# A third buffer for the expert weights, in the place of the normed rows, which are read back from DRAM; expert loops six long

## What is computed

```
h  = x @ W_in                                       # columns for HGRN2 heads and FoX heads
x  = LN1(alpha*x + W_out[HGRN2(h_hg) | FoX(h_fx)])
x  = LN2(alpha*x + MemCrossAttn(x, mem))            # 4 heads, 256 memory tokens
x  = LN3(alpha*x + HierMoE(x))
```

```
h = silu(xr @ w_gate[e]) * (xr @ w_up[e])           # 1024 -> 512, twice
y = h @ w_down[e]                                   # 512 -> 1024
```

## Time and profile before

| | us |
|---|---|
| median of 3 runs | 1876.02 |
| lowest and highest | 1871.96, 1881.76 |
| the profiled execution | 1861.41 |
| its span | 1859.6 |
| PE busy in the span | 1744.6 (94%) |
| VectorE busy | 745.7 (40%) |
| ScalarE busy | 326.0 (18%) |
| GpSimd busy | 195.9 (11%) |

### The profile page before, as it was taken

The page is one execution under the profiler, slowest core; times in us unless marked ns, Lnnn a source line. Parts: engine busy times, 40 slices in busy tenths (PEclk is TensorE's granted clock), DMA queues, the critical chain, the costliest instruction groups (busy, mean ns, idle before and its releaser), DMA issues. The chain is left out here.

```text
span 1859.6 us, 34670 instructions
## 1 busy us (share of the span) xinstructions
PE 1744.6 (94%) x15263; PEld 1095.6 (59%) x15263; DVE 745.7 (40%) x1172; ACT 326.0 (18%) x741; POOL 195.9 (11%) x190
## 2 busy tenths in 40 slices
PE   7999999999999999989998999849999999999976
PEld 4555566655666654445665666536666666666652
DVE  0212456623866753320003433574444433344337
ACT  1111224410344211110001111100111100111115
POOL 2100000000422000000000000032111111111003
PEclk9999989999999999989999999869999999999998
DMA  6171002001002040154101000349999999999957
GB/s 211 45 235 46 1 1 94 1 1 48 1 5 96 3 150 35 50 185 152 45 0 46 23 23 23 146 172 373 423 425 425 425 424 424 425 425 425 414 209 277
DMA packets 72870, 322.32 MB, mean 173 GB/s; under 512 B 14464, under 2 KB 29112, under 8 KB 59728
## 3 DMA queue, kind: packets, MB, share of 16 engines
q1 hardware_dynamic: 47840, 280.70, 37.6%
q10 hardware_dynamic: 17360, 22.03, 3.7%
q0 software_dynamic: 7584, 18.38, 2.7%
HBM read 288.05 MB, written 37.65 MB: 175 GB/s over the span
## 5 line engine op out<-in xcount | busy, mean ns | idle before, releaser
L852 PE MATMUL psum<-arena 128*32 128x256 f32 x6144 | 339.9, 381 | 20.8 <-issue 14.0
L852 PEld LDWEIGHTS psum<-arena 128*32 128x32 f32 x6144 | 230.7, 110 | 128.6 <-issue 33.8
L457 PE MATMUL psum<-arena 128*128 128x512 f32 x656 | 292.1, 604 | 7.6 <-DMA arena<-in_w_in 6.5
L1456 DVE COPY arena<-psum 128x512 f32<-128x512 f32 (+6 forms) x128 | 83.8, 663 | 382.9 <-PE psum L457 225.7
L457 PEld LDWEIGHTS psum<-arena 128*128 128x128 f32 x656 | 125.6, 194 | 160.5 <-issue 158.6
L672 PE MATMUL psum<-arena 128*128 128x352 f32 x576 | 177.9, 460 | 0.0
L861 PE MATMUL psum<-arena 128*32 128x256 f32 x3072 | 172.3, 379 | 0.5 <-DVE arena L1906 0.5
L442 PE MATMUL psum<-arena 128*128 128x352 f32 x576 | 172.3, 462 | 0.0
L1165 ACT ACTIVATE arena<-psum 128x128 f32<-128x128 f32 (+7 forms) x193 | 94.2, 497 | 351.3 <-PE psum L435 250.2
L442 PEld LDWEIGHTS psum<-arena 128*128 128x128 f32 x576 | 110.3, 192 | 61.8 <-issue 1.7
L861 PEld LDWEIGHTS psum<-arena 128*32 128x32 f32 x3072 | 116.3, 110 | 50.1 <-DVE arena L1906 1.0
(11 more groups left out here) (271 smaller groups left out, 1565.6 us busy)
## 6 DMA issues: line engine op xcount, KB each, us to landing
arena<-in_moe_w_down SPq DMA_DIRECT2D x34, 2048.0 KB, 21.8
arena<-in_moe_w_gate SPq DMA_DIRECT2D x34, 2048.0 KB, 16.6
arena<-in_moe_w_up SPq DMA_DIRECT2D x34, 2048.0 KB, 21.3
arena<-in_w_in SPq DMA_DIRECT2D x7, 2048.0 KB, 10.1
y_blocks<-arena ACTq DMA_DIRECT2D x136, 96.0 KB, 27.3
y_blocks<-arena ACTq DMA_DIRECT2D x1, 8448.0 KB, 46.0
arena<-in_x_prompt SPq DMA_DIRECT2D x9, 512.0 KB, 3.2
arena<-in_w_out SPq DMA_DIRECT2D x2, 2048.0 KB, 7.8
```

The costliest lines, as they stand in the source:

```text
L457: last = mm(ps[0:n, c * 512:(c + 1) * 512], lhs(k), rhs(k)[:, c * 512:(c + 1) * 512], start=(k == 0), stop=(k == KD - 1))
L852: last = mm(out, xeT[:, b, a, k, :], gu[b][:, :, k, j * P:(j + 1) * P], start=(k == 0), stop=(k == KD - 1))
L1456: take(V.tensor_copy(out, src), key)
```

## The change

Three weight buffers stand where two stood. The third begins at 24576 and ends at 36864, so it covers the last 512 floats of the mixer's region, all of `x1` and the norm parameters behind it. Expert e uses buffer e mod 3 for its weights; the buffers of its activations still alternate. The weights of expert 2 are loaded once the second norm's output is stored in DRAM and the last tile of it is transposed. Gate and up of expert e are issued when `gate_up` of expert e - 3 is done. When `down` of expert 29 is done, SyncE reads the rows back from `x2_dram` into `x1`, ahead of the overflow blocks' weights, and VectorE's tail waits for them (`x1_back`). Since two and three buffers repeat after six, the loops on TensorE and SyncE hold six experts (8 to 31, four rounds), with experts 0 to 7 written out. The small expert buffers and the LN3 parameters move.

```diff
-        EXP = [0, 12288]
+        EXP = [0, 12288, 24576]
...
-        ln3_par = view(R + 17920, "i n", i=2, n=D)
+        ln3_par = view(R + 23552, "i n", i=2, n=D)
...
+        x1_back = sem("x1_back")
...
-            def step(e, b, j, first=False):
+            def step(e, r, third_turn, first=False):
+                b, s = r % 2, r % 3
                 if not first:
                     pe.wait_ge(xt_ready, e + 1)
-                pe.wait_ge(wg_in[b], 16 * j + 16)
-                pe.wait_ge(wu_in[b], 16 * j + 16)
+                pe.wait_ge(wg_in[s], 16 * third_turn(r) + 16)
+                pe.wait_ge(wu_in[s], 16 * third_turn(r) + 16)
...
-            step(0, 0, 0, first=True)
-            step(1, 1, 0)
-            step(2, 0, 1)
-            with pe.Fori(1, NE // 2 - 1) as i:
-                step(2 * i + 1, 1, i)
-                step(2 * i + 2, 0, i + 1)
-            step(NE - 1, 1, NE // 2 - 1)
+            step(0, 0, lambda r: 0, first=True)
+            for e in range(1, 8):
+                step(e, e, lambda r: r // 3)
+            with pe.Fori(1, NE // 6) as i:
+                for r in range(2, 8):
+                    step(6 * i + r, r, lambda q: 2 * i + q // 3)
...
             sp.dma_start(gu[0][:, 1], up_w[0]).then_inc(wu_in[0], 16)
+            sp.wait_ge(ln_ready, 2 * NT)
+            sp.wait_ge(x2_stored, 16 * NT)
+            emptied(sp, ("X2T", NT - 1))
+            sp.dma_start(gu[2][:, 0], gate_w[2]).then_inc(wg_in[2], 16)
+            sp.dma_start(gu[2][:, 1], up_w[2]).then_inc(wu_in[2], 16)
+            sp.dma_start(wd[2], down_w[2]).then_inc(wd_in[2], 16)
...
+            def load_gate_up(e, s):
+                sp.wait_ge(gu_done, e - 2)
+                sp.dma_start(gu[s][:, 0], dyn(gate_w, e)).then_inc(wg_in[s], 16)
+                sp.dma_start(gu[s][:, 1], dyn(up_w, e)).then_inc(wu_in[s], 16)
+
+            def load_down(e, s):
+                sp.wait_ge(y_done, e - 2)
+                sp.dma_start(wd[s], dyn(down_w, e)).then_inc(wd_in[s], 16)
+
+            load_gate_up(3, 0)
+            for e in range(4, 8):
+                load_gate_up(e, e % 3)
+                load_down(e - 1, (e - 1) % 3)
+            with sp.Fori(1, NE // 6) as i:
+                for r in range(2, 8):
+                    load_gate_up(6 * i + r, r % 3)
+                    load_down(6 * i + r - 1, (r - 1) % 3)
+            load_down(NE - 1, (NE - 1) % 3)
+            sp.wait_ge(y_done, NE - 2)
+            sp.dma_start(x1[:, 0:8, :], x2_dram[0:SEQ, :].rearrange("(t p) n -> p t n", p=P)).then_inc(x1_back, 16)
+            sp.dma_start(x1[0:DEC, 8, :], x2_dram[SEQ:T, :]).then_inc(x1_back, 16)
...
             dve.wait_ge(ln3_loaded, 32)
+            dve.wait_ge(x1_back, 32)
```

More of the change, by code:

```diff
@@ L181, in build @@
         x2 = x1
-        EXP = [0, 12288]
+        EXP = [0, 12288, 24576]
         gu = [view(a, "m k n", m=2, k=KD, n=DE) for a in EXP]
         wd = [view(a + 8192, "k n", k=KE, n=D) for a in EXP]
[L185 to L190, removed]
-        ln3_par = view(R + 17920, "i n", i=2, n=D)
+        xe = view(R + 11776, "a s n", a=2, s=NS, n=256)
+        xeT = view(R + 13312, "a s k t", a=2, s=NS, k=KD, t=32)
+        hh = view(R + 14848, "s n", s=NS, n=P)
+        hhT = view(R + 15232, "a s k t", a=2, s=NS, k=KE, t=32)
+        ye = [view(R + 16000 + 768 * a, "s n", s=NS, n=256) for a in range(4)]
+        sg = view(R + 19072, "s n", s=NS, n=P)
+        ln3_par = view(R + 23552, "i n", i=2, n=D)
         rt = [R + 23552]
@@ L275, in build @@
         places_ready, row_ready = sem("places_ready"), sem("row_ready")
-        wg_in, wu_in, wd_in = ([sem(f"{n}_in{i}") for i in range(2)] for n in ("wg", "wu", "wd"))
+        wg_in, wu_in, wd_in = ([sem(f"{n}_in{i}") for i in range(3)] for n in ("wg", "wu", "wd"))
+        x1_back = sem("x1_back")
         xe_in = [sem(f"xe_in{i}") for i in range(2)]
@@ L840, in _, with gate_up @@
             B_Y = [psum[:, a * BANK:(a + 2) * BANK] for a in (4, 6)]
-            def gate_up(b, by_tile=False):
+            def gate_up(b, s, by_tile=False):
                 for a in range(NS):
@@ L851, in gate_up, with down @@
                             out = B_U[b][32 * j:32 * j + 32, a * 256:(a + 1) * 256].rearrange("p (m n) -> p m n", m=2)
-                            last = mm(out, xeT[:, b, a, k, :], gu[b][:, :, k, j * P:(j + 1) * P],
+                            last = mm(out, xeT[:, b, a, k, :], gu[s][:, :, k, j * P:(j + 1) * P],
                                       start=(k == 0), stop=(k == KD - 1))
                 return last
-            def down(b):
+            def down(b, s):
                 for a in range(NS):
```

12 lines of the change are left out of this document (6 added, 6 removed).

## The result

1903.28 us (median of 6 runs, 1901.08 to 1908.66) against 1879.86 us for the kernel before on the same chip: ratio 1.0144, 95% interval 1.0127 to 1.0161. The forecast was 1872, its range ended at 1889. The profiled execution of after took 1908.66 us (span 1906.6), the slowest of its runs. Its first expert starts 5.2 us later than in the profile before (1253.57 against 1248.39 us), but not by the change: from the issue of expert 1's down weights to the first gather it takes 41.0 us in both.

The account below looks back on a forecast made before the run. The weight stream was taken to bound the expert loop. Third buffer -16.0, read-back +11.3 and code traffic +2.4 gave -2.3 us at the first overflow block; -4 was taken, so 1876 - 4 = 1872 us, range 1862 to 1889.

Parts of the forecast that it names:

- the -16.0 for the third buffer: Expert loop: weights loaded ahead in the empty DMA stretch bring expert 31 16.0 us earlier.
- the cover: Before the first overflow block: TensorE, jumps included, is through at 1755.8, its weights land at 1763.8; 8 us remain.
- Profile against median: Whole kernel: the median of 1876.02 lies 14.6 us above the profiled execution, a difference carried over one to one.
- Jumps: TensorE's loop of six: three jumps back of 3.37 us, about 7 us showing in all, covered by the weight stream.
- Code traffic: DMA during the expert loop: code of 27 experts more is fetched, 1.03 MB, costing the weight stream 2.4 us.
- Read-back: Behind the last down weights: 4.33 MB of normed rows delay the first overflow block's weights by 11.3 us.
- y stores: Expert loop: landing grows from 44.1 to some 50 to 60 us, four buffers allow 62; costed at nothing, at most 5.
- Rival (a): Expert loop: jumps and refetched code decide, up to 9.3 us a jump, 8.2 showing; 1881 to 1892 us, chance 0.20.
- rival (c): Expert loop: no speed-up, held by ScalarE's stores or SyncE's queue; read-back costs 0 to 11; 1881 us, chance 0.08.

Follow-up runs that it names:

- before_again: The kernel before, unchanged, profiled once more: one execution, 1874.3 us.
- flat_noback: The changed kernel with all 32 experts written out on TensorE and without the read-back of the normed rows: ratio 1.0004 to the kernel before.
- spaced_three: The changed kernel with all 32 experts written out on TensorE and four GpSimd fills of 512 elements between gathers of experts 2 to 31: ratio 0.9969.
- spaced: The kernel before, small buffers at the change's places, with a GpSimd fill of 2048 elements between the gathers of experts 2 to 31: 1861.77 us, ratio 0.9936.
- six_two: The kernel before with TensorE's loop over six experts, still two weight buffers and no read-back: ratio 1.0103.
- flat_three: The changed kernel with all 32 experts written out on TensorE, so no jump back; SyncE's loop of six stays: ratio 1.0048 to the kernel before.
- moved: The kernel before with only the experts' small buffers and the LN3 parameters at the change's places: ratio 1.0002.

## Why the prediction was wrong

The step that failed is the first one, which the rest is built on: that TensorE takes 15.54 us for an expert and the weight stream is behind it. From it come both the -16.0 for the third buffer and the cover under which the jumps were to cost nothing. Step by step:

1. *Profile against median.* The profile was 14.6 us under the median and 10 under the fastest run, and I carried this over one to one. It was no offset: expert 31 comes 17.5 us later in before_again than in that profile (515.6 against 498.1), all of it in the expert loop. In the other executions an expert takes 16.5 to 16.6 us on TensorE, slightly more than its weights take (16.38 in the earlier trace rows), and there is nothing for a third buffer to shorten.
2. *Third buffer, -16.0.* Measured 0 with the pauses (flat_noback). Without them -4.8 to -6.2. Of the 16 us the refetched code takes 2.4 by the forecast's own price; the stream at 419 to 421 GB/s in spaced_three against 424 in spaced takes an estimated 3 to 6 more over 480 us. The rest is not settled. So the term was too large even where its condition held.
3. *Jumps, 3.37 us, 7 showing and covered.* Measured 6 us each, and 6 to 7 showing each, since the clock falls behind them; with TensorE the bound, nothing covers them. Cost: 18 to 19 us, shown from both sides (six_two adds them, flat_three takes them away). The price came from a single jump ahead; the jumps back took 1.8 times that. Even with 15.54 us an expert some 20 us of jumps would have used up the cover, 15 us in all (an estimate; no run has jumps without pauses). A slip besides: 3.37 - 1.35 leaves 2.0 us to show, not 2.2, and 9.3 leaves 7.9, not 8.2.
4. *Code traffic, 1.03 MB more.* Right, the last digit by luck: before holds six experts' code (0, 1, 2, the two of the loop, 31), so the code of 26 more is fetched, not of 27. Written out (flat_three) they move 0.97 MB more; the jumps of after bring the rest.
5. *Read-back, +11.3 on the first overflow block.* Right where the weights come last (10.7 and 11.5). With TensorE later, 5.6 to 6.2 of it show, and the clock falls in that wait: 8 us in all.
6. *y stores.* Not at the edge at all: their landing fell to a median of 2.3 us, against 27.3 in the earlier trace rows. Nor is it the full stream that makes it long: in spaced, whose engines are as full, it is 3.6 us, in moved 3.6, in before_again 12.0. It fell with the places of the small buffers; why is not shown.

The parts add up: 1.0103 for the loop and 1.0048 for the buffer with its read-back make 1.0151, against 1.0144 measured. Rival (a), the jumps decide, was right for that part; it was given 0.20, and its 1887 was short since it still counted a gain of the third buffer. That the third buffer is worth nothing, with the read-back still to pay, was rival (c), given 0.08, though neither ScalarE's stores nor SyncE's queue held the loop.

## What to carry to other kernels

A profiled execution that is faster than every timed run may not be the kernel one is changing: profile a second one before taking the bound from it, above all where two candidates lie within 6% of each other. A loop that is unrolled to turn buffers must still be one that the engine keeps: count its instructions (1152 were kept here, 1728 were not). And a buffer that takes the place of live data pays the bytes back at the end of the stream, where they are waited for (10.7 and 11.5 us here).

## What the runs showed that was not expected

Three indirect gathers issued 1.3 us apart make TensorE pause twice, about 0.45 us each, in the product that runs beside them, in every trace but the first; with 2.6 us of GpSimd's time between the gathers (3.6 us from start to start), or with plain loads, it doesn't pause. Spacing the gathers of thirty experts made the kernel 0.64% faster. The Trainium skill ("Trainium Architecture — The Big Picture", section "What this means for kernel authors") says that engines and DMA reach SBUF by separate sides that can't contend; what TensorE waits for in the pauses no run here shows, so it neither bears that out nor contradicts it.

Behind the jumps of after (a standstill of 4.7 us in the one shown) and the waits of 5.5 and 5.9 us before the first overflow block, TensorE's granted clock is at its lower level for a part of the next product: a mean of 0.60 over the 6.7 us behind the jump, of 0.58 and 0.77 over as much behind the two waits. Those products take 13.16, 13.31 and 12.02 us in place of 10.4.
